# A twelfth slot in the gather ring, 32 selection tiles in place of 8, and the last eighth of the query weights loaded again by halves

## The reference, cut to what matters

```python
def peer(h, wq, subkeys, u, v):
    chunks = h.reshape(-1, PEER_CHUNK, D_MODEL)          # 8 chunks of 128 tokens
    def one(xc):
        q = (xc @ wq).reshape(PEER_CHUNK, PEER_HEADS, 2, PEER_DKEY // 2)
        s = jnp.einsum('nhpd,hpkd->nhpk', q, subkeys).astype(jnp.float32)
        s1, i1 = lax.top_k(s[:, :, 0], PEER_TOPK)
        s2, i2 = lax.top_k(s[:, :, 1], PEER_TOPK)
        ...
        top_s, pos = lax.top_k(cand_s, PEER_TOPK)
        idx = jnp.take_along_axis(cand_i, pos, axis=-1)  # 8 heads x 16 experts per token
        g = jax.nn.softmax(top_s, axis=-1).astype(xc.dtype)
        act = jax.nn.gelu(jnp.einsum('nhkd,nd->nhk', u[idx], xc))
        return jnp.einsum('nhk,nhkd->nd', g * act, v[idx])
```

## Time and profile before

| | |
|---|---|
| timed runs | 3424.14, 3425.47, 3445.86 us; median 3425.47 us |
| span of the profiled execution | 3447.3 us |
| mean granted TensorE clock | 0.782 of full speed |
| busy in the span | PE 72%, DVE 59%, ACT 23%, POOL 61% |
| DMA | 1163.76 MB, mean 338 GB/s; the gathers' queue 1084.36 MB |
| first and last gather issued | 374.0 and 3430.5 us |

### The profile page before, as it was taken

The page is one execution under the profiler, slowest core; times in us unless marked ns, Lnnn a source line. Parts: engine busy times, 40 slices in busy tenths (PEclk is TensorE's granted clock), DMA queues, the critical chain, the costliest instruction groups (busy, mean ns, idle before and its releaser), DMA issues.

```text
span 3447.3 us, 29321 instructions
## 1 busy us (share of the span) xinstructions
PE 2466.8 (72%) x9222; PEld 1078.6 (31%) x9222; DVE 2047.0 (59%) x4621; ACT 785.3 (23%) x1888; POOL 2087.7 (61%) x2167
## 2 busy tenths in 40 slices
PE   7978977768676776677777867787767766533476
PEld 4844654324221432134222422143213422000011
DVE  4785786666655666656656566665665666565300
ACT  2265111122112221222122221222122212100121
POOL 6910254566666666666666666666666666666665
PEclk8989987886789667865797578956796688855699
DMA  8533499799999999999999999999999999999998
GB/s 319 179 140 113 142 337 358 288 358 362 349 371 367 360 364 367 362 368 358 364 367 375 361 364 372 372 358 366 364 361 370 361 355 359 372 379 368 364 367 323
DMA packets 335937, 1163.76 MB, mean 338 GB/s; under 512 B 40485, under 2 KB 51365, under 8 KB 333608
## 3 DMA queue, kind: packets, MB, share of 16 engines
q0 software_dynamic: 297792, 1084.36, 83.6%
q1 hardware_dynamic: 37994, 77.54, 6.3%
HBM read 1148.13 MB, written 13.63 MB: 337 GB/s over the span
## 4 chain that ended last, share of the span: by engine, by line
PE 29%; POOL 16%; issue 14%; another core or an unknown queue 13%; DMA 12%; DVE 11%; ACT 4%; SPq 1%; DVEq 0%; ACTq 0%; POOLq 0%
POOL arena L619 16%; DMA arena<-in_v,arena 9%; PE psum L2100 9%; DVE arena L1565 6%; PE psum L1931 4%; PE psum L1899 4%; DMA arena<-in_u,idx_u 2%; PE psum L2034 2%; PE psum L1920 2%; PE psum L1946 2%; PE psum L1781 1%; PE psum L1956 1%; PE psum L1980 1%; ACT arena L883 1%
## 5 line engine op out<-in xcount | busy, mean ns | idle before, releaser
L1565 DVE CUSTOM_DVE_ANT_0 arena<-arena,psum 128x1024 f32<-128x1024 f32 x1024 | 1215.6, 1218 | 413.3 <-DMA arena<-in_u,idx_u 379.4
L619 POOL DMA_INDIRECT arena<-in_u,idx_u x1024 | 960.0, 937 | 652.8 <-issue 267.8
L2100 PE MATMUL psum<-arena 128*32 128x512 f32 x4096 | 1013.0, 744 | 445.6 <-DMA arena<-in_v,arena 305.4
L619 POOL DMA_INDIRECT arena<-in_v,arena x1024 | 977.6, 955 | 522.1 <-issue 256.8
L2100 PEld LDWEIGHTS psum<-arena 128*32 128x32 f32 x4096 | 181.8, 124 | 1185.3 <-issue 1036.6
L960 ACT ACTIVATE arena<-arena 128x32 f32<-128x32 f32 x1024 | 277.6, 314 | 1166.4 <-PE psum L2100 580.1
L1899 PE MATMUL psum<-kT,arena 64*128 64x512 f32 (+1 forms) x384 | 252.4, 810 | 56.2 <-issue 26.9
L1920 PE MATMUL psum<-ident,arena 128*128 128x128 f32 x560 | 137.5, 378 | 174.5 <-issue 110.3
L1401 DVE TENSOR_REDUCE small<-psum 128x1 f32<-128x1280 f32 x64 | 95.4, 1491 | 278.4 <-remote 220.8
L1931 PE MATMUL psum<-v,arena 128*128 128x64 f32 x1120 | 230.4, 395 | 27.3 <-ACT arena L883 24.0
L2034 PE MATMUL psum<-wbig,arena 128*128 128x512 f32 x512 | 242.4, 628 | 4.5 <-issue 3.4
(11 more groups left out here) (268 smaller groups left out, 2154.9 us busy)
## 6 DMA issues: line engine op xcount, KB each, us to landing
arena<-in_u,idx_u POOLq DMA_INDIRECT x1024
arena<-in_v,arena POOLq DMA_INDIRECT x1024
arena<-in_w_mod POOLq DMA_DIRECT2D x20, 512.0 KB, 4.3
wbig<-in_wq SPq DMA_DIRECT2D x1, 7168.0 KB, 19.7
arena<-in_w_mod SPq DMA_DIRECT2D x12, 512.0 KB, 4.1
arena<-in_xin SPq DMA_DIRECT2D x5, 1024.0 KB, 9.6
arena<-in_w_mod SPq DMA_DIRECT2D x2, 2048.0 KB, 10.7
wbig<-in_w_mod SPq DMA_DIRECT2D x2, 2048.0 KB, 20.5
```

The source lines that it names most:

```text
L619: pool.indirect_dma_start(ring[:, r, :], None, t[table], bass.IndirectOffsetOnAxis(idx[:, j:j + 1], 0)).then_inc(got[r], 16)
L1565: V.tensor_tensor_reduce(ring[:, r, :], ring[:, r, :], hx_cur, 1.0, 0.0, ALU.mult, ALU.add, act_[:, j:j + 1]).then_inc(S["u_used"], 1)
L2100: ins = M(bank(4 + b)[QP * g:QP * g + QP, :], lhsT=sel[:, j % SELS, :], rhs=ring[:, r, 512 * b:512 * b + 512], start=(i == 0), stop=(i == ...
```

## The change

- `RING` goes from 11 to 12. Eleven slots stay where they were (`ARENA_SLOTS`), the twelfth is the first half of the last contraction tile of `wq` in `wbig`: columns 0 to 1023 of `wq[:, 7, :]`. The first gather into it (chunk 0, j = 11) also waits for chunk 0's four queries.
- `SELS` goes from 8 to 32. The selection tiles move to columns 1024 to 2047 of the same tile, 32 x 32 columns. `COLS_AHEAD`, by which ACT's program runs ahead of PE's, stays 8.
- That eighth of `wq` is in `wbig` for chunk 0's queries only. For chunks 1 to 7 it is loaded into `lc` and `att` (`wq_last`, 1024 columns), in two halves of 512 KB: the first after the chunk's output projection, the second, into the same memory, after its queries q(0) and q(1). PE waits for the first half at the last step of q(0), for the second at the last step of q(2).
- `load_l` now waits for all four queries of the chunk before, not for its output projection, since `lc` is taken until then.
- To make room for two more semaphores (`got11`, `wq_last_loaded`), four pairs are merged; each merged wait asks for the same events as before.

```diff
-RING = 11
+RING, ARENA_SLOTS = 12, 11
-SELS = 8
+SELS = 32
...
+        LC_AT = ATT_AT + 2 * KEYS + 4 * P
+        wq_last = arena[:, LC_AT:LC_AT + D]
...
+        sel = wq[:, KT - 1, D:2 * D].rearrange("p (s i) -> p s i", s=SELS)
+
+        def tile(r):
+
+            return ring[:, r, :] if r < ARENA_SLOTS else wq[:, KT - 1, (r - ARENA_SLOTS) * D:(r - ARENA_SLOTS + 1) * D]
...
             def load_l(n):
 
-                sp.wait_ge(S["out_half"], 2 * n)
+                wait(sp, "q_ready" if n > 1 else "out_half", 4 * n if n > 1 else 2)
...
+            def load_wq_last(n):
+
+                for half in range(2):
+                    if half:
+                        sp.wait_ge(S["q_ready"], 4 * n + 2)
+                    else:
+                        sp.wait_ge(S["out_half"], 2 * n + 2)
+                    sp.dma_start(wq_last, wqv[:, KT - 1, D * half:D * half + D]).then_inc(S["wq_last_loaded"], 16)
...
             for k in range(NX - 3):
+                load_wq_last(k + 2)
                 load_l(k + 3)
...
+                if c == 0 and j == ARENA_SLOTS:
+                    pool.wait_ge(S["q_ready"], 4)
...
-                        ins = M(bank(i), lhsT=hxT[:, kt, :], rhs=wq[:, kt, 512 * i:512 * i + 512],
-                                start=(kt == 0), stop=(kt == KT - 1))
+                        w = wq[:, kt, 512 * i:512 * i + 512]
+                        if n and kt == KT - 1:
+                            if i % 2 == 0:
+                                pe.wait_ge(S["wq_last_loaded"], 16 * (2 * n - 1 + i // 2))
+                            w = wq_last[:, 512 * (i % 2):512 * (i % 2) + 512]
+                        ins = M(bank(i), lhsT=hxT[:, kt, :], rhs=w, start=(kt == 0), stop=(kt == KT - 1))
```

More of the change, by code:

```diff
@@ L241, in layer @@
         hxT = view(KT * P, KT, P)
-        sel = view(SELS * QP, SELS, QP)
         hot = view(2 * QP)
@@ L331, in layer @@
             "gains_loaded", "wm_loaded0", "wm_loaded1", "wm_loaded2", "wm_loaded3", "wm_used",
-            "acc_loaded", "staged_in0", "staged_in1", "mod_summed", "mod_rows", "mod_out",
-            "silu_ready", "tanh_c", "g1_ready", "a2_ready", "b2_ready", "g2_ready",
-            "modT_ready", "kvl_loaded", "x_loaded", "x_sq",
+            "acc_loaded", "staged_in0", "staged_in1", "mod_summed", "mod_turned", "mod_out",
+            "silu_ready", "c_tanh_lam_exp", "g1_ready", "a2_ready", "b2_ready", "g2_ready",
+            "kvl_loaded", "x_loaded", "x_sq",
             "x_var", "x_sd", "xn_ready", "xT_first", "xT_ready", "hT_vec", "hT_act", "kv_ready", "lru_ready",
@@ L343, in layer @@
             "conv_done", "gates_r", "gates_i", "r_out", "i_out", "lru_a", "lru_m", "lru_i", "lru_s",
[L344 to L345 removed]
+            "lru_free", "lru_out", "lc_first", "lru_stored0", "lru_stored1", "z_sq", "z_tanh", "z_in", "z_done",
+            "wq_loaded", "wq_last_loaded", "wo_first", "wo_loaded", "g1_moved",
             "l_loaded", "xc_loaded", "scores_ready", "negmax_ready", "probs_ready", "sum_inverted",
@@ L349, in layer @@
             "q_out", "qT_ready", "qT_out", "s_first", "s_ready",  "gate_in", "gate_exp",
-            "idx_ready", "xm_moved", "idxT_ready", "idxT_copied", "hot_made",
+            "idx_ready", "xm_moved", "idxT_ready", "idxT_copied",
             "u_used", "v_used",
@@ L551, in _ @@
             load_x(1)
+            load_wq_last(1)
             load_l(2)
@@ L559, in _ @@
                 load_x(k + 3)
+            load_wq_last(NX - 1)
             for c in range(NX - 3, NX):
@@ L615, in _ @@
             ch.link(nc.gpsimd.memset(hot, 0.0))
-            nc.gpsimd.memset(hot[:, QP - 1:QP], 1.0).then_inc(S["hot_made"], 1)
+            nc.gpsimd.memset(hot[:, QP - 1:QP], 1.0).then_inc(S["filled"], 1)
             def gather(table, idx, j, r):
-                pool.indirect_dma_start(ring[:, r, :], None, t[table],
+                pool.indirect_dma_start(tile(r), None, t[table],
                                         bass.IndirectOffsetOnAxis(idx[:, j:j + 1], 0)).then_inc(got[r], 16)
@@ L691, in _ @@
             act.wait_ge(S["c_loaded"], 48)
-            A(csil, ccol, ACT.Tanh, scale=0.5).then_inc(S["tanh_c"], 1)
+            A(csil, ccol, ACT.Tanh, scale=0.5).then_inc(S["c_tanh_lam_exp"], 1)
             def x_norm(m):
@@ L801, in _ @@
             act.wait_ge(S["lam_ready"], 1)
-            A(lt[:, 1, :], lt[:, 0, :], ACT.Exp, scale=-1.0).then_inc(S["lam_exp"], 1)
+            A(lt[:, 1, :], lt[:, 0, :], ACT.Exp, scale=-1.0).then_inc(S["c_tanh_lam_exp"], 1)
             for m in range(1, NTOK // 2 - 1):
@@ L1085, in _ @@
             post(1, none)
-            act.wait_ge(S["hot_made"], 1)
+            act.wait_ge(S["filled"], 7)
             gelu(0)
@@ L1117, in _ @@
             V = nc.vector
-            dve.wait_ge(S["tanh_c"], 1)
+            dve.wait_ge(S["c_tanh_lam_exp"], 1)
             dve.wait_ge(S["filled"], 2)
@@ L1311, in _ @@
             V.tensor_copy(rowm, bank(4)).then_inc(S["mod_cols"], 1)
-            dve.wait_ge(S["modT_ready"], 1)
+            dve.wait_ge(S["mod_turned"], 1)
             dve.wait_ge(S["acc_loaded"], 32)
@@ L1343, in _ @@
             ch.step(V.tensor_scalar(lb, lb, 0.5, None, ALU.mult))
-            dve.wait_ge(S["lam_exp"], 1)
+            dve.wait_ge(S["c_tanh_lam_exp"], 2)
             ch.link(V.tensor_scalar(lt[:, 2, :], lt[:, 1, :], 2.0, None, ALU.add))
@@ L1564, in u_slots @@
                     r = landed(dve, c, u_place(c, j))
-                    V.tensor_tensor_reduce(ring[:, r, :], ring[:, r, :], hx_cur, 1.0, 0.0, ALU.mult, ALU.add,
+                    V.tensor_tensor_reduce(tile(r), tile(r), hx_cur, 1.0, 0.0, ALU.mult, ALU.add,
                                            act_[:, j:j + 1]).then_inc(S["u_used"], 1)
@@ L1615, in _ @@
             negmax(0, 0)
-            dve.wait_ge(S["mod_rows"], 1)
+            dve.wait_ge(S["mod_turned"], 2)
             dve.wait_ge(S["gains_loaded"], 48)
@@ L1729, in mod_sum @@
                                 start=True, stop=True)
-                ins.then_inc(S["mod_rows"], 1)
+                ins.then_inc(S["mod_turned"], 1)
             def keys(m, tt):
@@ L1835, in _ @@
                 ins = T(bank(6)[:, j * P:(j + 1) * P], rowm[:, j * P:(j + 1) * P], ident[:, :])
-            ins.then_inc(S["modT_ready"], 1)
+            ins.then_inc(S["mod_turned"], 1)
             pe.wait_ge(S["kvl_loaded"], 16)
@@ L2100, in v_slots @@
                         ins = M(bank(4 + b)[QP * g:QP * g + QP, :], lhsT=sel[:, j % SELS, :],
-                                rhs=ring[:, r, 512 * b:512 * b + 512], start=(i == 0), stop=(i == QP - 1))
+                                rhs=tile(r)[:, 512 * b:512 * b + 512], start=(i == 0), stop=(i == QP - 1))
                     ins.then_inc(S["v_used"], 1)
```

4 lines of the change are left out of this document (1 added, 3 removed).

## The result

The changed kernel takes 3473.17 us, the kernel before 3441.97 us (medians of 13 runs each). The ratio is 1.0079, 95% interval 1.0061 to 1.0097: slower by 0.8%. The forecast was 3394 us. Two of the three runs shown ahead of the prediction were the fastest of the 13, so its starting point, 3425.5 us, was 16.5 us low; against the median of 13 a gain of 31.1 us was forecast and a loss of 31.2 us measured.

A forecast was written before the change was run, and what follows sets the result against it. Gathers were taken to set the pace in lead and post, PE's attention in heads. Slot gains of 53.7 us less 17.6 for loads and 5 for chunk 1 gave 31.1 us less: 3425.5 to 3394 us, range 3330 to 3452.

The forecast's parts named there:

- If the slot is freed at the same moment as before: Twelfth slot: each late release holds POOL one gather later, shortening the wait by at most 1.24 us; gains 53.7 us in all.
- 18.6 us of gain in post: Post stretches: the twelfth slot shortens POOL's waits by 3.1 us, half the packets' bound, six times.
- the pause only moves: Rival: with a slot more, POOL stops one gather later and PE's packet comes later too; gain near 0, 3430 us, chance 0.18.
- the attention sets this pace, and POOL's waits here are an effect: Heads stretches: PE, busy 133 of 167 us, sets the pace, so an earlier free slot gains 0.
- Leads: Lead stretches: gathers set the pace; the twelfth slot gains 3.1 us in each of seven, 21.7 us.
- From 2970 us on: After the attention ends: the twelfth slot gains 6.2 us from 2970 to 3246 us and 7.2 us in the last chunk.
- 32 tiles at 0: Selection tiles: ACT need not wait for slot j - 8, but its work is not late, so the gain is set at 0.
- Loads, 17.6 us: Fourteen more loads of 512 KB take 1.25 us each of all DMA engines; the whole 17.6 us is charged.
- Chunk 1's bare load, 5 us: Chunk 1: no v slots stand between the queries, so the second half's load is bare, 4.3 to 5.8 us, taken as 5.
- The second half in chunks 2 to 7: PE's wait at q(2)'s last step is nothing: the load has some 7.4 us and needs 4.3, at most 5.8.
- The rival of the late half: Rival: the second half needs more than 7.4 us, PE stands at q(2)'s last step six times; 3473 us, chance 0.12.
- The limit of the DMA engines: Rival: gathers already run at the DMA limit, so loads cost 20 us and the slot gives nothing; 3451 us, chance 0.07.

The follow-up runs named there:

- e1_sels8: The changed kernel with 8 selection tiles again, ring of 12 and loads kept: 3483.78 us, ratio 1.0026 to the kernel before.
- e3_loads_alone: The changed kernel with a ring of 11 and 8 selection tiles, so only loads, their waits and merged signals remain: 3480.53 us, ratio 1.0019 to before.
- g4_both_sels8: The changed kernel with two added POOL waits, chunk 1's new order on PE and 8 selection tiles: 3474.88 us, ratio 1.0040 to before.
- g3_both_ring11: The changed kernel with two added POOL waits, chunk 1's new order on PE and a ring of 11: 3459.44 us, ratio 0.9994 to before.
- e2_ring11: The changed kernel with a ring of 11 again, 32 tiles and loads kept: 3481.04 us, ratio 1.0016 to before.
- e4_pause: The changed kernel plus a POOL wait before v gather 117 for the transposes of q(0) and q(1): 3472.09 us, ratio 0.9982 to before.
- e6_pause_traffic: e4_pause plus a 2 MB copy that POOL issues right before its added wait: 3468.01 us, ratio 1.0082 to before.
- e5_two_pauses: e4_pause plus a second POOL wait, before v gather 120, for the transposes of q(2) and q(3): 3440.91 us, ratio 0.9988 to before.
- f1_both_ring11: e5_two_pauses plus chunk 1's new order on PE and a ring of 11, on the chip where before took 3083.26 us: 3098.1 us, ratio 1.0054.

## Why the prediction was wrong, step by step

- **"If the slot is freed at the same moment as before"**: this is the step that failed, with all that hangs on it (18.6 us of gain in post). The slot isn't freed at the same moment, nor is anything else that PE signals. Where a stop of POOL's is spared, the signal may go undelivered: ACT saw the transposes 15.4 to 18.7 us after their end in place of 2.9 to 9.8, and POOL's wait before v gather 120 was 6.4 to 10.8 us long in all six chunks. POOL's standing in heads and post together went from 245.1 to 262.4 us, where 18.6 less were forecast, and adding stops at the two places gave back 35 us (15 us in the second set of runs, with chunk 1's new order besides). I had the mechanism as the rival "the pause only moves", and gave it 0.18 with a gain near 0. It was held down by "no mechanism in the rows ties PE's signals to POOL". The rows did: the earlier trace rows has POOL and ACT released 0.23 us apart, 2.63 us into POOL's pause. And the rival stopped short: it let the pause move, and did not ask who else reads these signals. ACT does, and PE waits for ACT.
- **Heads, "the attention sets this pace, and POOL's waits here are an effect"**: the gain was 0 as forecast, the reason wrong. PE busy 133 of 167 us looked like a bound; on the prompt chip the same work took 150 us, which isn't proof by itself, since its granted clock was 0.77 and not 0.61 and PE was busy for 123 us. What the rows fit is this: a head costs 12 gathers of 1.243 us and a stop of about 2.5 us in which PE's signals come: 17.4 us, which is what it took.
- **Leads**: 3.1 us each forecast, 10.6 us in the six of chunks 1 to 6 measured, 1.8 each. The right sign, the size off by nearly half, and the cause not the one named. The gain holds in all four traces of the changed kernel (78.3 to 79.9 us against 89.0), but it goes with the tiles: on the holding chips the leads of chunks 1 to 6 lose with 8 tiles 87.0 to 90.0 us, with eleven slots or twelve (before, e1_sels8, e3_loads_alone, g4_both_sels8); with 32 tiles and twelve slots 78.3 to 83.9, with 32 tiles and eleven slots 80.3 and 86.7 (g3_both_ring11, e2_ring11). (e4_pause, with one lead of 24.0 us, and e6_pause_traffic lie outside.) What the slot adds there can't be told from the scatter.
- **From 2970 us on**: 6.2 and 7.2 us forecast, -2.2 and 1.0 measured.
- **32 tiles at 0**: without the added waits their effect on the time can't be told (e2_ring11 against e3_loads_alone, 0.5 us). With them they give 15 us, and they shorten the leads, as above. An edit that "removes a wait" was priced by the wait, not by what the wait did to the engine beside it.
- **Loads, 17.6 us**: too much. With only the loads left, 0.19% (6.6 us by the ratio, -0.03 to 0.42%) for transfer and chunk 1 together, where 22.6 were charged. That they go into time in which POOL stands is likely and not shown.
- **Chunk 1's bare load, 5 us**: right. The row of PE shows 4.22 us, behind the signal of q(1), 5.9 us late itself, so that the load began at 642.04 for a product that ended at 636.1:

```profile
642.04 0.33 SPq L511 DMA_DIRECT2D arena<-in_wq  x1
...
646.33 2.08 PE L2060 MATMUL psum<-arena 128*128 128x512 f32 x2 [4.22 <-DMA arena<-in_wq]
```

  What came of it was larger: chunk 0's first v gathers of the second turn of the ring stood 26.8 us where they had stood 19.8.
- **The second half in chunks 2 to 7**: hidden, as forecast; PE waits for it nowhere but in chunk 1. The rival of the late half (0.12), which held all my chance for slower, is not what happened: the slower result came by a way that I had listed as harmless.
- **The limit of the DMA engines**: rejected rightly. Not even the prompt chip's 415 to 419 GB/s are shown to be such a limit: a gather of 524288 bytes every 1.243 us is 422 GB/s, so there the gathers stream at nearly the pace at which POOL issues them, and e6_pause_traffic has 474 GB/s over 3.5 us.
- **The numbers themselves**: the upper bounds of the gains add up to 165 us, not 166. In the earlier trace rows the last step of q(2) begins about 2102.15 us (half of the row's 1.98 us), 7.9 us behind ACT's move of q(1) and not 7.4. Neither matters to the result.

## What to carry to other kernels

When one engine's waits are "remote" and end together with those of another, ask what delivers the signal before pricing the wait: a stop that looks like waste may be the delivery, and then a deeper buffer can make the chain behind the signal later, not earlier. Test it by adding a stop at the place where the chain hands over; a wait that should cost time and gives some is the plainest proof. And compare the chips before the kernels: 360 us between two chips are more than ten times what the change did, and the changed kernel lay 0.45% above before in one set of runs and 0.98% in another, on chips of one kind.

## What the runs showed of the hardware

- PE's signals, while POOL issues an indirect DMA every 1.24 us, reach other engines late. The trace records 920 of the 1024 raises of `v_used` in before and 900 in after; if each is given the latest product that it can belong to, the raise comes 3.5 us (median) after the product's end in before and 3.9 us in after, and 8.2 and 9.0 us or more in a tenth of the cases. These are low estimates. Lags of 18 to 21 us stand above. After a stop of POOL's of 2.3 to 4.4 us the signals are there in most cases, several at once, and for the next few gathers they come without delay: q(3)'s end is seen within 0.1 us in e5_two_pauses, 3 us after the restart.
- DVE's signals aren't held: `u_used` is raised 0.011 to 0.013 us after the instruction's end in the same traces. Only 416 and 414 of its 1024 raises are recorded, but POOL bears it out. Take the gathers of before ahead of which POOL stood idle for 0.5 us or more: 23 needed a u slot whose use ended during that stop, and began 0.27 us (median) after that end. 202 needed a v slot; for 162 of them the product that freed it had ended before POOL stopped, and they began 8.6 us (median) after it.
- DMA traffic of 421 or 425 GB/s during a stop doesn't hold them (e4_pause, e6_pause_traffic).
- It depends on the chip. On one of them `v_used` is raised 0.015 us (median of 1024) after the product (f1_both_ring11) and the kernel before takes 3083 us; on all others here 3442 to 3477 us. The granted clock there is 0.84 to 0.86, and 0.78 to 0.79 on the others. What differs between these chips, and by what way POOL's issuing reaches PE's signals, no run here tells.
